# One change to a five-layer kernel on one core: the order of the first expert buffers, the layout of the expert loads, and the place of a gather

## The reference

```
h   = x + mixer(rmsnorm(x))
hn  = rmsnorm(h, norm_ffn)
g   = argmax over 4 groups of hn @ w_router_group        # one group for each token
top = 2 best of the 8 experts of that group, gates = p(group) * softmax(top)
for each of 32 experts e, over its tokens xb:
    y = (silu(xb @ w_gate[e]) * (xb @ w_up[e])) @ w_down[e]   # 1024x512, 1024x512, 512x1024
h  += sum over a token's two experts of gate * y
x2  = rmsnorm(h, final_norm)                              # goes on to the four further layers
```

## Time and profile before

| | |
|---|---|
| median of 3 runs | 1419.09 us (1418.38 to 1419.58) |
| the profiled execution | 1418.54 us, its span 1416.5 us |
| PE busy | 1150.6 us (81%) |
| DVE busy | 651.5 us (46%) |
| ACT busy | 421.8 us (30%) |
| bytes by DMA | 312.62 MB, mean 221 GB/s |

### The profile page before, as it was taken

How to read it: one execution, slowest core, us unless ns; L and a number is a source line. 1 busy time by engine, 2 the same in 40 slices (tenths; PEclk the granted TensorE clock), 3 DMA queues, 4 the chain that set the end, 5 groups by cost and what they waited for, 6 DMA issues and landing times. The chain is left out here.

```text
span 1416.5 us, 20647 instructions
## 1 busy us (share of the span) xinstructions
PE 1150.6 (81%) x8606; PEld 887.7 (63%) x8606; DVE 651.5 (46%) x1236; ACT 421.8 (30%) x644; POOL 6.1 (0%) x28
## 2 busy tenths in 40 slices
PE   4999899775665656556569999998899879899998
PEld 4999877422121221212139988888789779789887
DVE  4787478410100101010126468665458836454576
ACT  3554334100000000000025445462245433155353
POOL 1000000000000000000000000000000000000000
PEclk9999899899898989889889999999699988899999
DMA  8475213999999999999996533443134500046400
GB/s 275 126 240 197 101 60 121 400 409 409 410 410 410 409 410 410 409 410 410 409 357 210 179 119 120 138 160 119 38 141 142 156 2 3 1 127 181 143 27 30
DMA packets 119657, 312.62 MB, mean 221 GB/s; under 512 B 17059, under 2 KB 17290, under 8 KB 119578
## 3 DMA queue, kind: packets, MB, share of 16 engines
q1 hardware_dynamic: 116864, 310.78, 58.9%
q10 hardware_dynamic: 2714, 0.71, 0.2%
HBM read 310.42 MB, written 1.05 MB: 220 GB/s over the span
## 5 line engine op out<-in xcount | busy, mean ns | idle before, releaser
L1097 DVE TENSOR_TENSOR w_l<-ring,w_h 128x1024 fp32r<-128x1024 f32 x204 | 246.3, 1222 | 128.1 <-ACT w_h L638 126.6
L638 ACT ACTIVATE w_h<-ring 128x1024 fp32r<-128x1024 f32 x204 | 213.6, 1057 | 229.8 <-PE bank L2078 143.2
L2314 PE MATMUL bank<-ring,cm 128*32 128x512 f32 x960 | 144.5, 732 | 118.3 <-DMA ring<-in_w_gate 67.1
L2314 PEld LDWEIGHTS bank<-ring,cm 128*32 128x32 f32 x960 | 29.0, 121 | 232.0 <-DMA ring<-in_w_up 92.6
L2071 PE MATMUL bank<-hnT_h,w_h 128*128 128x256 f32 x992 | 143.7, 288 | 6.6 <-DVE cm L1061 3.1
L2075 PE MATMUL bank<-hnT_l,w_h 128*128 128x256 f32 x992 | 141.5, 286 | 0.0
L2078 PE MATMUL bank<-hnT_h,w_l 128*128 128x256 f32 x992 | 140.3, 284 | 0.0
L2071 PEld LDWEIGHTS bank<-hnT_h,w_h 128*128 128x128 f32 x992 | 129.3, 193 | 10.7 <-DVE cm L1061 3.6
L2075 PEld LDWEIGHTS bank<-hnT_l,w_h 128*128 128x128 f32 x992 | 130.2, 195 | 0.0
L2078 PEld LDWEIGHTS bank<-hnT_h,w_l 128*128 128x128 f32 x992 | 129.1, 194 | 0.4 <-DVE w_l L1097 0.4
L2335 PE MATMUL bank<-ring,cm 128*32 128x512 f32 x496 | 69.2, 684 | 48.3 <-DMA ring<-in_w_down 43.5
(11 more groups left out here) (414 smaller groups left out, 1413.9 us busy)
## 6 DMA issues: line engine op xcount, KB each, us to landing
ring<-in_w_down SPq DMA_DIRECT2D x62, 1024.0 KB, 16.1
ring<-in_w_gate SPq DMA_DIRECT2D x60, 1024.0 KB, 14.4
ring<-in_w_up SPq DMA_DIRECT2D x60, 1024.0 KB, 15.8
ring<-in_fox_w_in SPq DMA_DIRECT2D x32, 1024.0 KB, 9.1
ring<-in_w_in SPq DMA_DIRECT2D x22, 1024.0 KB, 8.7
ring<-in_gla_w_in SPq DMA_DIRECT2D x12, 1024.0 KB, 6.3
ring<-in_gdn_w_in SPq DMA_DIRECT2D x12, 1024.0 KB, 6.3
ring<-in_w_out SPq DMA_DIRECT2D x8, 1024.0 KB, 6.3
```

The costliest lines, as they stand in the source:

```text
L638: af(part(w_h, u, width), w, ACT.Copy).then_inc(s["high_ready"], 1)
L1097: v.tensor_tensor(part(w_l, u, width), w, part(w_h, u, width).bitcast(F32), ALU.subtract).then_inc(s["low_ready"], 1)
L2314: x = mm(bank[a][CAP * e:CAP * (e + 1), :], m_xg[:, 2 * b + r, CAP * e:CAP * (e + 1)], expert_of(w, e)[:, r * FF:(r + 1) * FF], start=(b = ...
```

## The change

- **First buffers** (FIRST_BUFFERS): steps 0 and 1 of the first quad in the ring, step 2 in cm_free, step 3 in vtm/sq, steps 4 and 5 in the ring, 6 and 7 in spare, 8 in spare/hnT, 9 to 11 in the ring. SP waits for ssd_m of 8 ahead of cm_free, for ssd_y of 8 ahead of vtm, for sq_summed of 4 ahead of sq.
- **Runs of 8 KB**: an up load takes four rows a partition (r=4), a down load two. A step's slot now holds two experts of four, each expert a half of its own, and PE works on pairs of slots: it waits for both, runs 32 matmuls, and raises the counter by two. The gather's and the transposes' columns are taken at the matching stride.
- **Gather**: behind the second pair of the up half (the first of w_up) in place of behind the last.
- **DVE**: the low parts of two weight units stand between the four xdt products and out_low behind them; before, the low parts stood ahead of the products and out_low in their middle.

```diff
+ROWS_UP, ROWS_DOWN = 4, 2
+FIRST_BUFFERS = ("ring", "ring", 0, 1, "ring", "ring", 2, 3, 4, "ring", "ring", "ring")
+FIRST_RING = [j for j in range(MOE_STEPS) if FIRST_BUFFERS[j] == "ring"]
...
-            return s["ring_used"], e + 1 + (EXTRA if e >= SLOTS else 0)
+            return s["ring_used"], 1 + (FIRST_RING[e] if e < len(FIRST_RING) else e + EXTRA)
...
-        up_v = [w.rearrange("(q j) (b p r) f -> q b p j (r f)", j=QUAD, p=P, r=2) for w in (w_gate, w_up)]
-        down_v = w_down.rearrange("(q j) (c p) n -> q c p j n", j=QUAD, p=P)
+        up_v = [w.rearrange("(q j) (b p r) f -> q b p j (r f)", j=QUAD, p=P, r=ROWS_UP) for w in (w_gate, w_up)]
+        down_v = w_down.rearrange("(q j) (c p r) n -> q c p j (r n)", j=QUAD, p=P, r=ROWS_DOWN)
...
-        extra = [[vtm[:].rearrange("p a b -> p (a b)"), sq[:].rearrange("p a b c -> p (a b c)")],
-                 [cm_free[:, 0:H], cm_free[:, H:2 * H]], [spare[:, 0:H], spare[:, H:2 * H]],
+        extra = [[cm_free[:, 0:H], cm_free[:, H:2 * H]],
+                 [vtm[:].rearrange("p a b -> p (a b)"), sq[:].rearrange("p a b c -> p (a b c)")],
+                 [spare[:, 0:H], spare[:, H:2 * H]],
...
-            if j < STEPS_UP:
-                return [(halves[h].rearrange("p (e x) -> p e x", e=QUAD // 2),
-                         up_v[j % 2][q, j // 2][:, 2 * h:2 * h + 2, :]) for h in (0, 1)]
-            return [(halves[h].rearrange("p (e f) -> p e f", e=QUAD // 2),
-                     down_v[q, j - STEPS_UP][:, 2 * h:2 * h + 2, :]) for h in (0, 1)]
...
+            i, e = j // 2, 2 * (j % 2)
+            w = up_v[i % 2][q, i // 2] if j < STEPS_UP else down_v[q, i - STEPS_UP // 2]
+            return [(halves[h].unsqueeze(1), w[:, e + h:e + h + 1, :]) for h in (0, 1)]
+
+        def pair_of(slot, q, j):
+
+            return slot(q, 2 * j) + slot(q, 2 * j + 1)
...
-                            k = j - SLOTS
-                            if q == 0 and 0 <= k < EXTRA:
+                            k = FIRST_BUFFERS[j] if q == 0 else "ring"
+                            if k != "ring":
                                 if k == 0:
-                                    sp.wait_ge(s["sq_summed"], 4)
+                                    sp.wait_ge(s["ssd_m"], 8)
                                 if k == 2:
                                     sp.wait_ge(s["unit_done"], UNIT_BASE["ssd_out"] + 4 * UNITS)
-                                if k == EXTRA - 1:
+                                if k == 4:
                                     sp.wait_ge(s["rt_done"], 1)
-                                for dst, src in moe_loads(extra[k], q, j):
+                                for h, (dst, src) in enumerate(moe_loads(extra[k], q, j)):
+                                    if k == 1:
+                                        sp.wait_ge(*((s["sq_summed"], 4) if h else (s["ssd_y"], 8)))
                                     sp.dma_start(dst, src).then_inc(extra_ready[k], 16)
...
-            low(UNIT_BASE["ssd_out"] + PARTS)
             xdt = vtm
             for k in range(4):
                 c, hf = k // 2, k % 2
-                if k == 2:
-                    out_low("ssd", 0, tiles(36, 2))
                 dve.wait_ge(s["ssd_xt_done"], k + 1)
...
                                 ALU.mult).then_inc(s["ssd_xt_used"], 1)
+                low(UNIT_BASE["ssd_out"] + PARTS + min(k, 2) - 2)
+            out_low("ssd", 0, tiles(36, 2))
...
-                        own = slice(2 * P * (k // 2) + k % 2, 2 * P * (k // 2 + 1), 2)
+                        own = slice(P * ROWS_UP * (k // ROWS_UP) + k % ROWS_UP, P * ROWS_UP * (k // ROWS_UP + 1), ROWS_UP)
...
-                for j in range(STEPS_UP):
-                    w, a, b = wait_slot(q, j), j % 2, j // 2
-                    for r in (0, 1):
+                for j in range(STEPS_UP // 2):
+                    w, a, b = pair_of(wait_slot, q, j), j % 2, j // 2
+                    for r in range(ROWS_UP):
+                        k = ROWS_UP * b + r
                         for e in range(QUAD):
...
-                    x.then_inc(release, 1)
-                gather(g + 1, it + 1)
+                    x.then_inc(release, 2)
+                    if j == 1:
+                        gather(g + 1, it + 1)
...
-                for c in range(STEPS_DOWN):
-                    w = wait_slot(q, STEPS_UP + c)
-                    for n in (0, 1):
-                        for e in range(QUAD):
...
-                    x.then_inc(release, 1)
+                for j in range(STEPS_DOWN // 2):
+                    w = pair_of(wait_slot, q, STEPS_UP // 2 + j)
+                    for r in range(ROWS_DOWN):
+                        c = ROWS_DOWN * j + r
+                        for n in (0, 1):
+                            for e in range(QUAD):
...
+                    x.then_inc(release, 2)
```

More of the change, by code:

```diff
@@ L236, in build @@
         w_gup = sb("w_gup", [16, BLK])
-        g_ffn = sb("g_ffn", [P, KD // 2, 2])
+        g_ffn = sb("g_ffn", [P, KD // ROWS_UP, ROWS_UP])
         cols = sb("cols", [16, 8])
@@ L537, in _ @@
                                 for j in range(MOE_STEPS):
-                                    for dst, src in moe_loads(ring_halves(0), q, j):
+                                    for dst, src in moe_loads(ring_halves(j % 2), q, j):
                                         sp.dma_start(dst, src).then_inc(ov_ready, 16)
-                                    sp.wait_ge(ov_used, (p - 1) * (NQ * MOE_STEPS) + q * MOE_STEPS + (j + 1))
-                                    sp.sem_inc(s["sp_turn"], 1)
+                                    if j % 2:
+                                        sp.wait_ge(ov_used, (p - 1) * (NQ * MOE_STEPS) + q * MOE_STEPS + (j + 1))
+                                        sp.sem_inc(s["sp_turn"], 1)
             for k in range(4):
@@ L2309, in pe_quad @@
                 pe.wait_ge(s["moe_h"], it + 1)
-                for j in range(STEPS_UP):
-                    w, a, b = wait_slot(q, j), j % 2, j // 2
-                    for r in (0, 1):
+                for j in range(STEPS_UP // 2):
+                    w, a, b = pair_of(wait_slot, q, j), j % 2, j // 2
+                    for r in range(ROWS_UP):
+                        k = ROWS_UP * b + r
                         for e in range(QUAD):
-                            x = mm(bank[a][CAP * e:CAP * (e + 1), :], m_xg[:, 2 * b + r, CAP * e:CAP * (e + 1)], expert_of(w, e)[:, r * FF:(r + 1) * FF],
-                                   start=(b == 0 and r == 0), stop=(b == KD // 2 - 1 and r == 1), tile_position=(0, CAP * e))
-                    x.then_inc(release, 1)
-                gather(g + 1, it + 1)
+                            x = mm(bank[a][CAP * e:CAP * (e + 1), :], m_xg[:, k, CAP * e:CAP * (e + 1)], w[e][:, r * FF:(r + 1) * FF],
+                                   start=(k == 0), stop=(k == KD - 1), tile_position=(0, CAP * e))
+                    x.then_inc(release, 2)
+                    if j == 1:
+                        gather(g + 1, it + 1)
                 pe.wait_ge(s["moe_sg"], it + 1)
@@ L2326, in pe_quad @@
                 for c in range(STEPS_DOWN):
-                    x = tr(b4(2)[:, c, :], m_h[:, c * P:(c + 1) * P], ident[:])
+                    own = slice(2 * P * (c // 2) + c % 2, 2 * P * (c // 2 + 1), 2)
+                    x = tr(b4(2)[:, c, :], m_h[:, own], ident[:])
                 x.then_inc(s["moe_ht"], 1)
@@ L2330, in pe_quad @@
                 pe.wait_ge(s["moe_acc"], it + 1)
-                for c in range(STEPS_DOWN):
-                    w = wait_slot(q, STEPS_UP + c)
-                    for n in (0, 1):
-                        for e in range(QUAD):
-                            x = mm(bank[3 + n][CAP * e:CAP * (e + 1), :], m_ht[:, c * P + CAP * e:c * P + CAP * (e + 1)],
-                                   expert_of(w, e)[:, n * BLK:(n + 1) * BLK], start=(c == 0), stop=(c == STEPS_DOWN - 1),
-                                   tile_position=(0, CAP * e))
-                    x.then_inc(release, 1)
+                for j in range(STEPS_DOWN // 2):
[4 more added lines that the diff above has]
+                            for e in range(QUAD):
+                                x = mm(bank[3 + n][CAP * e:CAP * (e + 1), :], m_ht[:, c * P + CAP * e:c * P + CAP * (e + 1)],
+                                       w[e][:, r * D + n * BLK:r * D + (n + 1) * BLK], start=(c == 0), stop=(c == STEPS_DOWN - 1),
+                                       tile_position=(0, CAP * e))
+                    x.then_inc(release, 2)
                 pe.wait_ge(s["moe_gtc"], it + 2)
@@ L2349, in first_slot @@
             def first_slot(q, j):
-                if SLOTS <= j < SLOTS + EXTRA:
-                    pe.wait_ge(extra_ready[j - SLOTS], 32)
-                    return extra[j - SLOTS]
-                n = RING_BASE["moe"] + (j if j < SLOTS else j - EXTRA)
+                k = FIRST_BUFFERS[j]
+                if k != "ring":
```

(3 more changed lines are left out.)

6 lines of the change are left out of this document (2 added, 4 removed).

## The result

The changed kernel takes 1424.75 us (median of 20 runs, 1416.46 to 1431.87), the one before 1419.38 (20 runs, 1411.13 to 1424.88): ratio 1.0042, 95% interval 1.0025 to 1.0059. It is slower, by 3.6 to 8.4 us. The profiled execution took 1426.08 us, span 1424.0; before 1418.54, span 1416.5.

A forecast was written before the change was run, and what follows sets the result against it. Expert stage bound by DMA, its weight bytes at 409.6 GB/s. From the profiled 1418.54 us, -5.0 (stream start) + 3.2 (tail) + 0 (rate) gives 1416.7; the median lies 0.55 higher, so 1417.3, range 1411.5 to 1424.

The forecast's parts named there:

- the gather's price: Expert stage, gather between matmul pairs: 3.9 us to the next start, as in the kernel before.
- the rate: Expert weight loads: going from 4 KB to 8 KB runs leaves the DMA rate unchanged, 0 us.
- the start of the stream: Start of the expert loop: step 1 of the second group lands at 303.7, not 308.69, 5.0 us sooner.
- The bound of 4 us each way: Expert weight loads: 8 KB runs make the kernel at most 4 us faster or 4 us slower.
- S = 272.88 - 1.6 = 271.3.: PE's start of the expert loop: VectorE's new order in the scan brings it 1.6 us sooner, to 271.3.
- Whether pairs keep the stream full ... No loss.: Expert loop: PE may take 7.8 us from landing to release; a pair takes 5.1 us, so nothing is lost.
- the second rival: Expert loop, after gathers and at group starts: the ring starves by pairs, 24 us, 1443 (1427 with a third); chance 0.12.
- The tail: After the last landing: a pair of 5.1 us replaces a step of 1.92, 3.2 us more.
- The clock falls well: Rival at loop start and tail: PE starts 2.5 us sooner, tail 1.6 to 2.4, total 1415.2; chance 0.15.
- the rate rival: Expert weight loads: longer runs raise the DMA rate, saving 4 to 5 us, total 1412.8; chance 0.11.

The follow-up runs named there:

- slots one by one: Changed kernel with adjacent gather columns, PE waiting for, using and releasing single slots, and tanh waiting for six steps, not seven: 1409.26 us, ratio 0.9937 to before.
- the flat gather: Changed kernel with the normed tokens stored so that the gather reads adjacent columns, not every fourth: 1416.78 us, ratio 0.9995 to before.

## Why the prediction was wrong

The forecast was 1417.3 us, from 1411.5 to 1424.0; 1424.75 lies above its upper end. The step that turned about the same time into a slower kernel is the gather's price, which was carried over from before to another stride: without that stride the kernel is at 0.9995, where the forecast was. Pairs cost at least as much, since with slots one by one it falls on to 0.9937. Two further terms failed by more than it and partly cancel: the rate (taken at 0, measured at 12 us to the good) and the start of the stream (5.0 us sooner forecast, 5.0 later measured). The steps one by one:

- **The gather's price, "a gather 3.9", taken over from before.** The change reads its columns at stride 4, and I priced no operation of it anew. At full clock a weight load went from 196 to 329 ns, the gather from 4.04 to 7.73 us: about 6.7 us over the whole kernel (after against the flat gather). Two gathers stand on the path that sets the stream's start.
- **"Doubling the run brought nothing, so I take 0."** Failed, to the good: 422 against 410 GB/s, 12 us where alone. From 2 and 4 KB running at one rate I concluded to the next doubling, and even the premise is weak. The 410 of the 2 KB runs comes from windows of 2 us in the middle of bursts of 2 MB. In before's later layers (800 to 1110 us) the two 1 MB loads of such a burst land 2.61 to 2.69 us apart in 14 of 19 cases, 390 to 402 GB/s; with 4 KB it is 2.56 us in the loop and 2.59 for the pair issued at 231.09. So by my estimate 2 KB was slower by some 2% all along. The bound of 4 us each way was too narrow too: it was drawn from the fall of the DMA share and not from anything that limits the rate. The rule of the Trainium skill ("DMA: Bandwidth & Descriptors", Why small descriptors are slow) gives 1.1% from 4 to 8 KB by the estimate in the prediction: the right sign, but the runs show 2.9%. The 2.3% that the prediction worked out from the Trainium skill for 2 to 4 KB, and found not borne out, agrees with 2.65 against 2.59 us.
- **"S = 272.88 - 1.6 = 271.3."** It was 274.41. The early product was there (idle 1.58 and 1.47 us where 3.85 had been, spreads 2.2 us sooner counted from the transposes), and over seven against five profiles the mean gain is 2.1 us at the residual's transposes and 1.6 at the first expert matmul. But the profile of before, from which I counted, is one of the two quick ones of five, against which 0.8 us was left at 249 us. As after reached the transposes 0.8 us later, that was used up, and the slow gather (7.73 for 5.87) did the rest. That 1.6 comes out as the mean too is partly luck, since the gathers in that mean differ.
- **"5.0 us sooner", the start of the stream.** It came 5.0 us later (16th landing, table). The buffers filled as forecast, but the pause was 268.5 to 281.2 us, 12.7 us for the 6.5 of the sum. PE began 3.1 us later than summed, its first pair took 5.16 us and not 3.54 (granted clock 0.50 from 274.4 to 276.0), and more followed while the second gather stood between the pairs. With a gather of before's stride the gain was 0.6 us instead. Alone the order of the buffers is worth nothing, 0.9996 and 0.9940 against 0.9937: it moves transfer ahead and then waits for PE.
- **"Whether pairs keep the stream full ... No loss."** Failed. The forecast allowed 7.8 us from a landing to its release at 410 GB/s, which is 9.94 - 2.4 = 7.5 at 422. This rests on the need to issue 0.7 + 1.4 = 2.1 us ahead of a landing, and that term was too small: with the flat gather pairs came late at leads up to 4.7 us, which is 5.1 us from landing to release. At 410 GB/s pairs left leads of 4.5 us and more and lost next to nothing, at 422 leads fell to 2.0 us, and the loop lost 4.1 us in after and 7.9 with the flat gather, nearly all at leads of at most 4.7; step by step, at 7.1 and more, nothing was lost. Each pair's first part also ran cold for longer than the half that I had taken (6.29 us, not 5.1, at 446.21). It is the second rival's mechanism and place, but its sum of 24 us was far too high. Why a lead of 4 us is too short at one time and enough at another is open.
- **The tail, "3.2 us more".** Mis-sized: 4.2, since both halves of the last pair ran cold for most of their length (6.16 us). Behind it came what no step named: 3.7 us up to the next projection, of which 2.2 are a wait on "issue". Most kernels with pairs or with single slots of two experts show 0.9 to 3.1 us there, but the one with everything but the 8 KB runs shows none (its wait of 1.9 us stands behind VectorE); 8 KB alone 0.75, VectorE alone 0.2, before none. What the sequencer waits for was not shown.
- **"The clock falls well", and the rate rival (0.11).** The clock did not fall well: pairs behind a wait took 5.0 to 6.4 us. The rival of the rate was true in its mechanism and still not the outcome, because it was summed alone. Effects by parts: -0.9% (runs), 0 (buffers), -0.2% (VectorE), +0.4% (pairs), 0 (gather's place), +0.5% (stride) give -0.2%; measured is +0.4%. Each part is uncertain by 0.2 to 0.4% and their sum by some 0.7%, so by the times alone the remaining 0.6% could be noise. That the parts meet badly is seen in the traces: alone the longer runs shorten the 80 landings by 11.9 us, with pairs (everything but 8 KB against the flat gather) by 5.1.

## What to carry to other kernels

A change of a layout in DRAM has a second reader: look up every operation that indexes by the same factor, and price its new stride, before the transfer itself. A stream that is faster needs its buffers released sooner; check release against landing at the new rate, at the coarsest place of the loop, and measure how far ahead of a landing the next load has to be issued, from the landings and not from the rate just behind an issue. And when filling buffers earlier is the idea, ask what releases the first of them: where that is the consumer's start, the early transfer turns into a pause.

## What the runs showed of the hardware

- DMAs of 128 partitions with runs of 8 KB move 422 GB/s, with 4 KB 410. With 2 KB, windows of 2 us show up to 410, but two queued loads of 1 MB land 2.65 us apart (median of the 14 in before's later layers), 396 GB/s, against 2.56 and 2.485 with 4 and 8 KB in the loops. With 64 partitions and 16 KB it is 213.
- At 422 GB/s, in the flat gather's loop, 12 of the 24 pairs that were issued at most 4.7 us ahead of the landing before them came late, by 0.2 to 1.3 us; of the 15 that were issued earlier none did.
- Weight loads of 128x128 in f32 take 192 ns at stride 1, 196 at 2, 329 at 4 (medians at mostly full clock); so stride 2 is nearly free and 4 is not. At the granted clock of 0.50 they take 331 to 333 ns at strides 1 and 2 and 329 at 4: there stride 4 costs nothing.
- Sixteen matmuls of 128x512 over 32 columns each take 1.92 us spread on four column groups, 3.63 on two, both at clock 1.00. Used step by step, with idle stretches of 1.35 us, PE stayed at a granted clock of 1.00 (2.4 GHz) through the loop; by pairs, idle for 3 to 7 us ahead of most of them, it came back at the lower level, and a pair took 5.0 to 6.4 us in place of 3.64.
- Identical code reaches the same point of one program up to 2.8 us apart (81.0 or 83.8 us) and comes to the scan's transposes 166.6 to 169.5 us from the start: an earlier start of 1 to 2 us can't be read from one profile of each kernel.
